# Starting the next stage on half of its tokens at six sublayer boundaries of a two-block transformer kernel

## What is computed

```python
x = layer_norm(ALPHA * x + mix, ln_mix_g[i], ln_mix_b[i])
x = layer_norm(ALPHA * x + conv_ffn(x, ...), ln_ffn_g[i], ln_ffn_b[i])
...
x = x + g1 * y                                   # second block
h = rmsnorm(x, norm2_g) * (1.0 + sc2) + sh2
x = x + g2 * (square(relu(h @ w_in)) @ w_out)
```

## Time and profile before

| | us |
|---|---|
| median of 3 runs (lowest, highest) | 2811.45 (2811.03, 2812.35) |
| the profiled execution | 2811.43 |
| its span, first to last instruction | 2809.5 |
| PE busy | 2783.7 (99%), 13890 matmuls |
| POOL, DVE, ACT busy | 1140.6, 1303.3, 1081.2 |
| mean granted TensorE clock | 0.998 of full |

### The profile page before, as it was taken

One profiled execution on the slowest core, in us unless ns is written; L12 is line 12 of the kernel. 1 busy time (PEld: TensorE's weight loads), 2 busy tenths in 40 slices (PEclk: granted clock), 3 DMA queues, 4 the chain that ended last, 5 costly groups with the idle time before them and its releaser, 6 DMA issues.

```text
span 2809.5 us, 37915 instructions
## 1 busy us (share of the span) xinstructions
PE 2783.7 (99%) x13890; PEld 2287.7 (81%) x13890; DVE 1303.3 (46%) x1516; ACT 1081.2 (38%) x1574; POOL 1140.6 (41%) x472
## 2 busy tenths in 40 slices
PE   9999999999999999999989999999999999999999
PEld 8788888888878788888877788888888888888887
DVE  4157568863441658874276651123423642411232
ACT  3443443343332544333345643334333223432332
POOL 4333434444434024444435035444344434444443
PEclk9999999999999999999999999999999999999999
DMA  5322238742333027753321023332243322233332
GB/s 160 90 69 74 90 103 267 239 140 88 99 88 95 9 76 232 244 169 102 97 73 45 2 74 106 97 105 98 86 135 94 90 78 103 90 92 96 104 98 75
DMA packets 319812, 299.95 MB, mean 107 GB/s; under 512 B 16268, under 2 KB 251224, under 8 KB 319576
## 3 DMA queue, kind: packets, MB, share of 16 engines
q1 hardware_dynamic: 304680, 236.70, 28.2%
q10 hardware_dynamic: 15024, 61.75, 6.3%
HBM read 296.30 MB, written 2.11 MB: 106 GB/s over the span
## 4 chain that ended last, share of the span: by engine, by line
PE 46%; issue 36%; POOL 16%; DVE 1%; ACT 0%; POOLq 0%; DVEq 0%; ACTq 0%
POOL wlo L558 16%; PE ps L2034 8%; PE ps L2035 8%; PE ps L2036 8%; PE ps L1892 6%; PE ps L1894 6%; PE ps L1893 6%; PE ps L2319 1%; PE ps L2255 1%; PE ps L2284 1%; PE ps L2394 1%; PE ps L2065 0%; PE ps L2067 0%; PE ps L2066 0%; PE ps L1897 0%
## 5 line engine op out<-in xcount | busy, mean ns | idle before, releaser
L558 POOL TENSOR_TENSOR wlo<-raw,whi 128x1024 fp32r<-128x1024 f32 x444 | 1115.3, 2515 | 1630.6 <-ACT whi L616 1630.3
L1892 PE MATMUL ps<-xhi,whi 128*128 128x512 f32 x1824 | 718.0, 394 | 0.3
L1894 PE MATMUL ps<-xhi,wlo 128*128 128x512 f32 x1824 | 710.3, 389 | 0.0
L1893 PE MATMUL ps<-xlo,whi 128*128 128x512 f32 x1824 | 709.9, 389 | 0.0
L616 ACT ACTIVATE whi<-raw 128x1024 fp32r<-128x1024 f32 x444 | 466.3, 1052 | 288.9 <-PE ps L2036 167.8
L2034 PE MATMUL ps<-whi,ahi 128*128 128x512 f32 x1184 | 461.4, 390 | 0.7 <-DVE alo L1396 0.7
L2036 PE MATMUL ps<-whi,alo 128*128 128x512 f32 x1184 | 460.7, 389 | 0.0
L2035 PE MATMUL ps<-wlo,ahi 128*128 128x512 f32 x1184 | 460.6, 389 | 0.0
L1892 PEld LDWEIGHTS ps<-xhi,whi 128*128 128x128 f32 x1824 | 342.5, 188 | 73.1 <-issue 3.2
L1894 PEld LDWEIGHTS ps<-xhi,wlo 128*128 128x128 f32 x1824 | 342.3, 188 | 71.7
L1893 PEld LDWEIGHTS ps<-xlo,whi 128*128 128x128 f32 x1824 | 342.6, 188 | 71.0 <-issue 1.4
(11 more groups left out here) (282 smaller groups left out, 2858.0 us busy)
## 6 DMA issues: line engine op xcount, KB each, us to landing
adaraw<-in_ada_w ACTq DMA_DIRECT2D x64, 768.0 KB, 6.1
raw<-in_ffn_w_up SPq DMA_DIRECT2D x88, 512.0 KB, 4.0
raw<-in_mlp_w_in SPq DMA_DIRECT2D x64, 512.0 KB, 4.0
raw<-in_mlp_w_out SPq DMA_DIRECT2D x64, 512.0 KB, 3.7
raw<-in_gmlp_w_in SPq DMA_DIRECT2D x48, 512.0 KB, 3.8
raw<-in_sc_ssm_w_in SPq DMA_DIRECT2D x44, 512.0 KB, 3.8
raw<-in_ffn_w_down SPq DMA_DIRECT2D x44, 512.0 KB, 3.6
raw<-in_fox_w_in SPq DMA_DIRECT2D x24, 512.0 KB, 3.8
```

Source lines behind the costliest of these rows:

```text
L558: pool.tensor_tensor(wlo[:, j], raw[:, j], whi[:, j].bitcast(F32), ALU.subtract).then_inc(w_lo, 1)
L1892: pe.matmul(out, lh, rh, start=start, stop=False)
L1893: pe.matmul(out, lh, rl, start=False, stop=False)
L1894: return pe.matmul(out, ll, rh, start=False, stop=stop)
```

## The change

Six boundaries (`PARTED`) take the four early blocks in two parts: tokens 0 to 255 (tiles 0 and 1), then 256 to 511. PE transposes part 0 before (3,0) at LayerNorm boundaries and before (3,1) at RMSNorm ones, then runs the first three units on blocks 0 to 3 of part 0 as matmuls of 256 columns, transposes part 1 before the third unit's block 3, and repeats on part 1. Blocks 4 to 7 follow at 512 columns. At q = 6 the first two units run blocks 0 to 3 on tiles 0 and 1, then on tiles 2 and 3, at 512 columns as before. The transposes of the identity go at these six. ACT's scratch output of the squares moves from `junk` to `nrm`, and `gate` to another address.

```diff
+PARTED = (1, 2, 3, 5, 6, 7)
+PART = (slice(0, 256), slice(256, 512))
...
+    def act_xt_part(act, q, scale, bias, h):
+        c = PART[h]
+        for k in range(4):
+            act.wait_ge(xt_tp, XT0[q] + 4 * h + k + 1)
+            if k >= 2:
+                act.wait_ge(xt_lo, XT0[q] + 4 * h + k - 1)
+            act.activation(xf[:, k % 2, c], ps[:, k, c], ACT.Identity, scale=scale(k), bias=bias(k)).then_inc(xt_ev, 1)
...
     def act_ln_tail(...):
-        for t in range(NT):
-            act_ln_std(act, r, t)
-            if t == 1:
-                act_next_whi(act, name, 2)
+        act_ln_std(act, r, 0)
+        act_ln_std(act, r, 1)
+        act_xt_part(act, r + 1, scale, bias, 0)
+        act_ln_std(act, r, 2)
+        act_next_whi(act, name, 2)
+        act_ln_std(act, r, 3)
         load_gb(act, gb, g_ap, b_ap)
+        act_xt_part(act, r + 1, scale, bias, 1)
+        act_xt(act, r + 1, scale, bias, 4)
...
     def act_rms_tail(...):
         for t in range(NT):
-            if t == 2 and early:
-                act_next_whi(act, name, 2)
+            if t == 2:
+                if early:
+                    act_next_whi(act, name, 2)
+                act_xt_part(act, r + 1, norm_scale(s), norm_shift(s), 0)
...
+    def dve_xt_part(dve, q, h):
+        for k in range(4):
+            dve.wait_ge(xt_ev, EV0[q] + 4 * h + k + 1)
+            dve.tensor_copy(xhi[:, k, c], xf[:, k % 2, c]).then_inc(xt_hi, 1)
+            dve.wait_ge(xt_hi, XT0[q] + 4 * h + k + 1)
+            dve.tensor_tensor(xlo[:, k, c], xf[:, k % 2, c], xhi[:, k, c].bitcast(F32), ALU.subtract).then_inc(xt_lo, 1)
     def dve_xt(dve, q, resid=None, k0=0):
+        if resid is not None:
+            dve_resid(dve, resid, 3)
...
     def dve_ln_tail(...):
+        for h in range(2):
+            dve_ln_moments(dve, r, name, h and 3)
+            if not h:
+                dve_ln_moments(dve, r, name, 1)
+            for t in (2 * h, 2 * h + 1):
+                dve_ln_inverse(dve, r, t)
+                norm(t, 0)
+            if not h:
+                dve_ln_moments(dve, r, name, 2)
+            dve_xt_part(dve, r + 1, h)
+        for t in range(NT):
+            norm(t, 1)
+        dve_xt(dve, r + 1, resid=r, k0=4)
...
     def dve_rms_tail(...):
+        tile(0)
+        tile(1)
+        for t in range(2):
+            inverse(t)
+            norm(t, 0)
+        tile(2)
+        dve_xt_part(dve, 5 + s, 0)
+        tile(3)
+        for t in range(2, 4):
+            inverse(t)
+            norm(t, 0)
+        dve_xt_part(dve, 5 + s, 1)
+        for t in range(NT):
+            norm(t, 1)
+        dve_xt(dve, 5 + s, k0=4)
...
     def pe_f(...):
+            for h in range(2):
+                for k in range(4):
+                    pe.wait_ge(xt_lo, XT0[q] + 4 * h + k + 1)
+                    for e in range(2):
+                        if not h and k == 0:
+                            pe.wait_ge(w_lo, S + e + 1)
+                            pe.wait_ge(res_add, 8 * q - 3 + e)
+                        product(e, k, PART[h])
+                if h:
+                    for k in range(4, KD):
+                        pe_xt_late(pe, q, k)
+                for k in range(4):
+                    if not h and k == 0:
+                        pe.wait_ge(w_lo, S + 3)
+                        pe.wait_ge(res_add, 8 * q - 1)
+                    if not h and k == 3:
+                        pe_xt_part(pe, q, 1)
+                    product(2, k, PART[h])
+            for k in range(4, KD):
+                pe.wait_ge(xt_lo, XT0[q] + 4 + k + 1)
+                for e in range(3):
+                    ins = product(e, k, slice(0, T), k == KD - 1)
```

More of the change, by code:

```diff
@@ L82 @@
 GU_SLOTS = 4
+PARTED = (1, 2, 3, 5, 6, 7)
+XT0 = [0]
+for _q in range(8):
+    XT0.append(XT0[-1] + (12 if _q in PARTED else 8))
+EV0 = [_n - 8 for _n in XT0]
+PART = (slice(0, 256), slice(256, 512))
 NRM_ORDER = ((0, 0), (1, 0), (0, 1), (2, 0), (3, 0), (1, 1), (2, 1), (3, 1))
@@ L1653, in dve_rms_tail, with tile @@
         dve.tensor_scalar(mv[:, :, 1], sumsq[:, :, 0], 1.0 / D, EPS, ALU.mult, ALU.add).then_inc(half_sq, 1)
-        for t in range(NT):
+        def tile(t):
             wait_tile(dve, 4 + s, name, t)
             dve_gated_tile(dve, s, 1, t)
[L1657 to L1664, removed]
+        tile(0)
[11 more added lines that the diff above has]
+        for t in range(NT):
             norm(t, 1)
+        dve_xt(dve, 5 + s, k0=4)
     def dve_last_tail(dve, s, name):
@@ L1674, in dve_qkv @@
         dve.wait_ge(qkg_in, 48)
-        dve.wait_ge(xt_lo, 40)
+        dve.wait_ge(xt_lo, XT0[5])
         for z in range(2):
@@ L1948, in pe_table, with pe_f @@
                 ins.then_inc(tab_tp, 1)
-    def pe_f(pe, name, freed, q=None, first=(), after=None):
+    def pe_f(pe, name, freed, q=None, after=None):
         S, n = U0[name], NUNITS[name]
@@ L1963, in unit @@
             ins.then_inc(unit_done, 1)
-        for s, v in first:
-            pe.wait_ge(s, v)
         if q == 0:
@@ L2019, in pe_f, with pe_t_unit @@
                     unit(i * RING + j, j)
-    def pe_t_unit(pe, start, e, j, bank0, lh, ll, first, blocks=None):
+    def pe_t_unit(pe, start, e, j, bank0, lh, ll, first, blocks=None, tiles=range(NT), done=True, mid=None):
         slot = (start + j) % RING
@@ L2027, in pe_t_unit @@
         for k in range(2):
+            if mid and k:
+                mid()
             if blocks is not None:
                 pe.wait_ge(xt_lo, blocks + k + 1)
-            for t in range(NT):
+            for t in tiles:
                 out = ps[:, bank0 + t]
@@ L2071, in pe_t_tail @@
                 ins.then_inc(tile_done, 1)
-            if q and q != 4 and t == 2 and i:
-                pe_xt_tile(pe, q, 0)
-        if q:
-            for t in range(0 if q == 4 else 1, NT):
+            if q in PARTED and (t, i) == ((2, 1) if q < 4 else (3, 0)):
+                pe_xt_part(pe, q, 0)
+        if q == 4:
+            for t in range(NT):
                 pe_xt_tile(pe, q, t)
@@ L2382, in pe_gm, with unit @@
         S, SU = U0["gv"], U0["gu"]
-        def unit(e0, j, b, blocks=None):
-            pe_t_unit(pe, S, e0 + j, j, 4 * b, xhi[:, 2 * j:2 * j + 2], xlo[:, 2 * j:2 * j + 2], j == 0, blocks=blocks)
+        def unit(e0, j, b, **kw):
+            pe_t_unit(pe, S, e0 + j, j, 4 * b, xhi[:, 2 * j:2 * j + 2], xlo[:, 2 * j:2 * j + 2], j == 0, **kw)
         def spatial(cc):
@@ L2396, in spatial @@
             ins.then_inc(gm_mm, 1)
+        pe.wait_ge(res_add, 46)
+        unit(0, 0, 1, blocks=XT0[6], tiles=(0, 1), done=False)
+        unit(0, 1, 1, blocks=XT0[6] + 2, tiles=(0, 1), done=False, mid=lambda: pe_xt_part(pe, 6, 1))
         pe.wait_ge(res_add, 48)
-        for j in range(4):
-            unit(0, j, 1, blocks=48 + 2 * j)
-            if j == 0:
-                for k in range(4, KD):
-                    pe_xt_late(pe, 6, k)
+        unit(0, 0, 1, blocks=XT0[6] + 4, tiles=(2, 3))
+        for k in range(4, KD):
+            pe_xt_late(pe, 6, k)
+        unit(0, 1, 1, blocks=XT0[6] + 6, tiles=(2, 3))
+        for j in range(1, 4):
+            if j > 1:
+                unit(0, j, 1, blocks=XT0[6] + 4 + 2 * j)
             if j == 1:
-                pe.wait_ge(xt_ev, 48)
+                pe.wait_ge(xt_ev, EV0[7])
                 pe.wait_ge(ws_in, 16)
```

116 lines of the change are left out of this document (59 added, 57 removed).

## The result

The changed kernel takes 2822.78 us (2820.89 to 2824.28, 6 runs) against 2811.44 (2810.95 to 2812.35) for the kernel before: a ratio of 1.004, 95% interval 1.0029 to 1.0051, so 11.3 us slower. The forecast was 2818.1, within 2807 to 2829, slower with a chance of 0.52. Of all executions reported here one was in a slow state (e3_rms_whi_behind, 3102.1 us, where the others took 2813 to 2817); it is left out.

The account below looks back on a forecast made before the run. The prediction took PE, at 99% of the span, to bound the kernel, its share hiding padding. LayerNorm +5.7, RMSNorm +2.2 and q = 6 -1.2 made +6.7 on 2811.45: 2818.1 us, range 2807 to 2829.

Parts of the forecast that it names:

- LayerNorm, +1.9 each: At q = 1, 2, 3: removed padding is outweighed by waits and half steps, +1.9 us each, +5.7 together.
- The meeting of block 7 with `wlo`: LayerNorm boundaries: POOL's wlo starts 0.4 us ahead of block 7's subtraction, which waits 2.2 us, and PE with it.
- A1: All six boundaries: no meeting of DVE with POOL decides; 2807.9 us, chance 0.12.
- A2: LayerNorm boundaries: only block 7 escapes its meeting with POOL, by the margin of 0.4 us; 2811.5 us, chance 0.16.
- a copy of q = 1: q = 2 was costed on q = 1's clock, like every LayerNorm boundary: +1.9 us.
- RMSNorm, +1.1 each: At q = 5, 7: first cast waits for wlo, PE stalls 2.1 us; +1.1 us each, +2.2 together.
- the 0.2 for switches: Allowance at LayerNorm and RMSNorm boundaries for the half steps' excess and switches of shape: 0.2 us each.
- q = 6: Boundary with 512-column matmuls: PE starts at once on tiles 0 and 1, third unit waits for wlo; -1.2 us.
- Half steps at 0.12: PE's 256-column matmuls in the parts: 0.12 to 0.13 us each, weight load not holding them up.
- rival C: A 256-column half step on PE costs the full 0.227 us; 2839 us, chance 0.08.
- Rival D: Padding gone, PE's clock falls at four waits of 2.1 us, about 2 us each; around 2826 us, chance 0.09.
- Rival E: PE, not DVE, sets the pace; waits vanish and each boundary gives 3.3 of its 4.4 us; 2791 us, chance 0.10.

Follow-up runs that it names:

- e3: e1 with the third unit's whi moved behind part 0's four xf pieces at q = 5 and 7; 2814.56 us, ratio 1.0012.
- e1: The changed kernel with the load of wf_raw issued ahead of part 1 again, as before the change; 2818.67 us, ratio 1.0026.
- e10: The kernel before with only the load of wf_raw moved behind q = 2's eight xf blocks; 2811.27 us, ratio 1.0.
- e5: The kernel before without its transposes of the identity at the six boundaries, kept at q = 4; 2823.93 us, ratio 1.0044.
- e6: e1 plus e3 and e4, three norm early at LayerNorm boundaries, third unit's whi right behind part 0's pieces at all six; 2805.90 us, ratio 0.9978.
- e7: e6 with q = 1, 2 and 3 as in the kernel before, padding included, so parts only at q = 5, 6, 7; 2803.95 us, ratio 0.9973.
- e8: e1 with 16 transposes of the identity ahead of block 7 at q = 1, 2, 3 and the first product at q = 5, 7; 2816.59 us.
- e4: e1 with two of the second half's four norm made ahead of part 1's half blocks at all six boundaries; 2812.33 us, ratio 1.0005.
- e2: e1 with shift(1) behind block 7 instead of ahead of it at LayerNorm boundaries; 2816.23 us, ratio 1.0017.

## Why the prediction came out as it did

- **LayerNorm, +1.9 each: right in mechanism and nearly in size.** At q = 1 the forecast had the first product near 393.6, waits of 0.6, 0.6, 1.0 and 2.2, and the fourth unit at 418.4 (with 0.2 more for the excess); measured are 393.63, waits of 0.3, 0.4, 0.8 and 1.9, and 418.31. Price +1.6. The meeting of block 7 with `wlo`, by a margin of 0.4 (measured 0.38), was there: rivals A1 and A2 fall. The rule behind it, that a DVE operation with all operands in SBUF waits for a running `wlo`, was drawn from one row and is too wide: the statistics at 394.75 did not wait.
- **q = 2 was not a copy of q = 1, and this is the step that failed.** The sum took 1.9 for it and nothing behind. The whole diff moves the load of `wf_raw` past the `xf` blocks, and a DMA that is moved on ACT's queue has to be costed like any other operation: its latency became a wait of 1.74 on ACT. With the fourth unit's split late, q = 2 was spared the meeting before block 7 (-0.4 instead of +1.9), and then lost 7.5 further on. Net 7.1 where 1.9 stood: 5.2 more than forecast. e1 and e10 show that it took the load and the parts together.
- **RMSNorm, +1.1 each: measured +0.6.** The cast took 2.10 and PE waited 2.00, both as said; the wait for tile 3 was 1.0 (1.2), the one before the late transposes 0.6 (0.8), and the 0.2 for switches did not show. **q = 6**: -1.5 for -1.2, with the third unit waiting 1.51 (1.7).
- **Half steps at 0.12: right, rival C is out.** 256-column matmuls with a weight load each ran 0.12 apart throughout, against the estimated 0.22 that the prediction worked out from the Trainium skill's page "TensorE: Matmul & The Clock Gate" ("LDWEIGHTS (loading the stationary operand)" with the line in "The mechanism" that ties the overlap to a different row group). The same section of that page also lets a weight load run ahead when it goes to the background weight buffer, and the measured 0.12 agrees with that half.
- **Rival D, the clock, had 0.09 and was partly true**: about 2.9 us in the profiled execution, but behind the wait of 4.3 and at none of the waits of 2 that it named (in e1 it fell behind two of them). At q = 4 and the attention behind it, where the half clock comes in two pieces in place of one, the profiled execution has 0.8 more. That is not shown to be the change's: e10, whose boundaries are those of the kernel before, is 0.6 below that kernel there, and e1, parts and all, is level from q = 4 on. The prediction also took the half clock at q = 4 to follow an idle time of 3.12; in that trace PE had idled 6.22 before 1421.68, and the window 1418 to 1422 already reads 0.51. e5 shows what the mechanism can cost: 12.7 us if no work replaces the padding, the largest effect of any run here.
- **Rival E (faster) falls** as argued: DVE's chain of part 1 and four `norm` (399.20 to about 403.9) outlasts PE's 24 half steps. Gains of the size that it had in mind, 3.3 each, came near at q = 5 to 7 only: 2.2, 3.5 and 2.2 in e6 and e7, once ACT's and DVE's orders were mended.

Of the profiled executions' +10.7, boundaries are 2.4 (forecast 6.7), the load with its half clock 7.5 (0), q = 4 and the attention 0.8 (0). The sum was 2.0 too much at q = 1, 3, 5, 7 and 6 together, and 5.2 and 0.8 too little elsewhere. That the time is inside the range is in part luck: the largest single loss stood in no term and no rival, and the range was wide enough to take it in. With the load back in its place e1 measured 2818.67, close to the forecast 2818.1, but of its 7.3 some 2.8 are half clock (e1 against e8 at q = 2 and 3), for which the sum had no term.

What stays open: why the clock falls behind one wait of 2 us and not behind the next. At q = 1 the changed kernel, e1 and e4 kept it, e6 lost it, with waits alike (1.91, 1.90, 1.88 and 1.90). The pieces at q = 4 were not followed up either. Parts at a single LayerNorm boundary were not tried.

## What to carry to other kernels

When work is reordered, follow every instruction that changes place on each queue, loads first: the one costly move here was one line that the description of the change doesn't mention, and it cost only together with another shift. Filling one engine's gap hands the bound to the next (here DVE, which waits for POOL's `wlo` and POOL for it), so order that engine first; two `norm` moved into an idle 1.3 us were worth 5 us. And padding that keeps TensorE's clock is removed only where useful work takes its place: in e7 the waits left at q = 5 to 7 are 1.3 us at most and the clock stayed at 1.00 there, while behind waits of about 2 us it fell in some places of e1, e3 and e6.

## What the runs showed of the hardware

- Removing 204 transposes of the identity, some 24 us of PE's busy time, from gaps in which PE had nothing else to do made the kernel 12.7 us slower (e5), through stretches at a granted clock of 0.50 at each of the six boundaries, where PE idles twice, for 1.6 to 2.2 us each.
- The same wait of about 2 us was followed by such a stretch in some places and executions and not in others, so a kernel with unpadded waits has a time that the sum of its waits doesn't give (e1 against e8: 2.1 us).
- Casts, `norm` and elementwise operations on two SBUF operands on DVE, and POOL's `wlo`, lock each other out by whole operations: two `shift` that need 2.35 together took 6.74 behind runs of `wlo`, a `wf_lo_t` of 0.28 took 2.42, a cast of 128x256 took 2.10 instead of 0.29, and POOL's `wlo` grew from 2.4 to 3.3 when it came second (e2, 412.33). DVE's statistics kept their 0.69 beside a `wlo` (394.75). In the Trainium skill, "SBUF — State Buffer", section "Who interferes with whom", calls this an exclusive lock held for a whole instruction; these rows agree.
